# Block 2's opening shared out over three engines, fewer waits around attention, and a weight stream in five slots of eight atoms

## The reference, cut to what matters

```python
for i in range(DEPTH):                      # DEPTH = 2
    a_l = modulate(rms_norm(h_lat, norm_g[i, 0]), sh1, sc1)
    a_c = modulate(rms_norm(h_ctx, norm_g[i, 0]), csh1, csc1)
    # i == 0: y = pool_mix(a) for both sides; i == 1: attention, latents ask, both sides answer
    h_lat = h_lat + g1 * y_l
    h_lat = h_lat + g2 * sq_relu_mlp(modulate(rms_norm(h_lat, norm_g[i, 1]), sh2, sc2))
    # i == 0: the same for h_ctx
return rms_norm(h_lat, final_g)
# pool_mix: moving average over tokens minus the token, then a 256x256 product per group of columns
```

## Time and profile before

| | us |
|---|---|
| median of 3 runs | 1922.51 (1916.69 to 1923.26) |
| the profiled execution's own time | 1923.36 |
| its span, first to last instruction | 1921.5 |
| PE busy | 1795.2 (93%) |
| POOL busy | 1131.5 (59%) |
| ACT busy, DVE busy | 868.5 (45%), 834.1 (43%) |
| mean granted clock of PE | 0.963 of full |
| stream | 463 fetches of 640 KB, 3.9 us from issue to landing |

### The profile page before, as it was taken

One profiled execution on the slowest core, in us unless ns is written; L12 is line 12 of the kernel. 1 busy time (PEld: TensorE's weight loads), 2 busy tenths in 40 slices (PEclk: granted clock), 3 DMA queues, 4 the chain that ended last, 5 costly groups with the idle time before them and its releaser, 6 DMA issues.

```text
span 1921.5 us, 32487 instructions
## 1 busy us (share of the span) xinstructions
PE 1795.2 (93%) x13080; PEld 1630.0 (85%) x13080; DVE 834.1 (43%) x1970; ACT 868.5 (45%) x1364; POOL 1131.5 (59%) x611
## 2 busy tenths in 40 slices
PE   6889999999998899999999879999999889889997
PEld 5878899999998788999999757777787677679997
DVE  7677435313365775443334852121212445542223
ACT  5535546444665355464446753222323333454443
POOL 5666568778786665778887314343433323147884
PEclk9889999999998999999999979999999889989999
DMA  6453355655464534656555224433445433125552
GB/s 244 144 212 114 124 208 176 239 179 180 164 219 141 203 124 137 235 177 222 180 190 193 97 96 164 151 137 137 151 165 205 178 142 114 33 83 175 182 180 90
DMA packets 70167, 311.51 MB, mean 162 GB/s; under 512 B 7680, under 2 KB 9984, under 8 KB 69760
## 3 DMA queue, kind: packets, MB, share of 16 engines
q1 hardware_dynamic: 68400, 306.47, 46.4%
q10 hardware_dynamic: 1616, 2.95, 0.5%
HBM read 308.34 MB, written 1.05 MB: 161 GB/s over the span
## 4 chain that ended last, share of the span: by engine, by line
PE 76%; DVE 8%; POOL 4%; ACT 3%; DMA 3%; issue 3%; DVEq 2%; ACTq 0%; SPq 0%
PE bank L909 23%; PE bank L913 22%; PE bank L912 22%; POOL wlo L869 4%; DMA raw<-in_stream 3%; PE bank L924 2%; DVE split_acts L1756 1%; ACT whi L1306 1%; PE bank L932 1%; PE bank L1076 1%; PE bank L1106 1%; PE bank L1090 1%; DVE acts L2334 0%; ACT bank L1351 0%; PE bank L1238 0%
## 5 line engine op out<-in xcount | busy, mean ns | idle before, releaser
L869 POOL TENSOR_TENSOR wlo<-raw,whi 128x320 fp32r<-128x320 f32 (+1 forms) x607 | 1131.3, 1888 | 769.0 <-ACT whi L1306 768.2
L909 PE MATMUL bank<-split_acts,whi 128*128 128x256 f32 (+1 forms) x3540 | 1086.0, 307 | 53.3 <-DVE split_acts L1756 31.9
L912 PE MATMUL bank<-split_acts,whi 128*128 128x256 f32 (+1 forms) x3540 | 1068.8, 302 | 0.0
L913 PE MATMUL bank<-split_acts,wlo 128*128 128x256 f32 (+1 forms) x3540 | 1068.3, 302 | 0.0
L909 PEld LDWEIGHTS bank<-split_acts,whi 128*128 128x128 f32 x3540 | 685.2, 194 | 110.5 <-issue 48.6
L913 PEld LDWEIGHTS bank<-split_acts,wlo 128*128 128x128 f32 x3540 | 686.4, 194 | 22.0
L912 PEld LDWEIGHTS bank<-split_acts,whi 128*128 128x128 f32 x3540 | 687.0, 194 | 20.9
L1306 ACT ACTIVATE whi<-raw 128x1280 fp32r<-128x1280 f32 x367 | 464.3, 1268 | 510.8 <-PE bank L909 253.5
L2387 DVE SCALAR_TENSOR_TENSOR acts<-bank,acts 128x256 f32<-128x256 f32 x104 | 47.4, 482 | 230.8 <-PE bank L913 230.8
L2401 DVE TENSOR_SCALAR acts<-bank 128x512 f32<-128x512 f32 (+1 forms) x64 | 35.7, 558 | 212.3 <-PE bank L913 212.3
L1756 DVE TENSOR_TENSOR split_acts<-bank,split_acts 128x256 fp32r<-128x256 f32 (+1 forms) x204 | 94.4, 463 | 53.4 <-ACT split_acts L1447 24.3
(11 more groups left out here) (265 smaller groups left out, 1562.9 us busy)
## 6 DMA issues: line engine op xcount, KB each, us to landing
raw<-in_stream SPq DMA_DIRECT2D x463, 640.0 KB, 3.9
acts<-in_x SPq DMA_DIRECT2D x1, 1024.0 KB, 6.0
acts<-in_ctx ACTq DMA_DIRECT2D x1, 1024.0 KB, 7.8
acts<-in_const ACTq DMA_DIRECT2D x1, 1024.0 KB, 5.2
out<-acts SPq DMA_DIRECT2D x8, 128.0 KB, 2.1
acts<-in_const SPq DMA_DIRECT2D x1, 708.0 KB, 8.4
acts<-in_p ACTq DMA_DIRECT2D x2, 256.0 KB, 4.0
acts<-in_const ACTq DMA_DIRECT2D x1, 320.0 KB, 3.1
```

Of the source, the lines that this page charges most:

```text
L869: last = nc.gpsimd.tensor_tensor(wlo[slot][:, cols], raw[source][:, cols], whi[slot][:, cols].bitcast(F32), ALU.subtract)
L909: first = nc.tensor.matmul(out_ap, w_hi, hi_act(k), start=(k == 0), stop=False)
L912: nc.tensor.matmul(out_ap, w_hi, lo_act(k), start=False, stop=False)
L913: last = nc.tensor.matmul(out_ap, w_lo, hi_act(k), start=False, stop=(k == k_tiles - 1))
```

## The change

It has four parts.

1. The stream's chunks hold 8 atoms, in five slots (`AHEAD`, `SLOTS_AHEAD` and `FREE_SLOTS` = 4). All of it is 555 chunks instead of 463, and an "ada" chunk has no empty atoms left. The count of a layer's tiles is no longer rounded up.
2. Opening: the context's modulated tile lies in bank 7, one buffer, and x's squares in two banks. ACT also writes x times gain (`xg_ready`), POOL multiplies by the reciprocal, two tiles for each `pool_out` (`first_out`). The squares of the two norms behind the pooling have eight buffers and are summed by PE in eight matmuls. In the other norms of block 2 the eighth square goes to PE alone.
3. Attention layer: for a q tile ACT splits only what the tile needs, squares, and splits ahead after that. The split ahead of a norm's root stands two tiles later (t == 3). The first scores wait for key head 0 alone, those of unit 4 on for all keys, and V's copies are shared by DVE (0, 1) and ACT (2, 3).
4. The other lines replace the number of a tile's bank by one that counts through the layers.

```diff
-CHUNK_ATOMS = 10
-RING = 4
+CHUNK_ATOMS = 8
+RING = 5
-AHEAD = 3
-SLOTS_AHEAD = 3
+AHEAD = 4
+SLOTS_AHEAD = 4
...
-        pooled_sq = [sq2[:, 512 + i * 256:768 + i * 256] for i in range(4)]
+        pooled_sq = [sq2[:, i * 256:(i + 1) * 256] for i in range(KT)]
-        r_first = bank[7][:, 0:256]
+        r_first = var_first
-        x_squares = [bank[5], bank[6], bank[7]]
+        x_squares = [bank[5], bank[6]]
-        c_mod = [pr2[:, 512:768], pr2[:, 768:1024]]
+        c_mod = bank[7][:, 0:256]
+        last_sq = squares[:, 0:512]
...
+            def normed_latents():
+                pool.wait_ge(xg_ready, KT)
+                pool.wait_ge(first_ready, 1)
+                for k in range(KT):
+                    nc.gpsimd.tensor_tensor(side(h, k, 1), side(h, k, 1), r_first, ALU.mult).then_inc(first_out, 1)
...
             for n in range(N_SPLITS):
                 lo_parts(n, 4 if n in SHORT_PIECES else 1)
+                if n + 1 == first_splits:
+                    normed_latents()
...
+                    elif t[1:3] == (0, 1):
+                        for k in range(KT):
+                            pe.wait_ge(pooled_sq_ready, t[3] * KT + k + 1)
+                            last = nc.tensor.matmul(o, ones[:, 0:128], pooled_sq[k], start=(k == 0),
+                                                    stop=(k == KT - 1))
                     else:
                         norms += 1
-                        pe.wait_ge(sq2_used, norms * KT)
-                        src = sq2[:, cols]
-                    last = nc.tensor.matmul(o, ones[:, 0:128], src, start=True, stop=True)
+                        pe.wait_ge(sq2_used, norms * (KT - 1))
+                        nc.tensor.matmul(o, ones[:, 0:128], sq2[:, cols], start=True, stop=False)
+                        pe.wait_ge(sq2_ready, norms * KT)
+                        last = nc.tensor.matmul(o, ones[:, 0:128], last_sq[:, cols], start=False, stop=True)
...
-                if u in (0, 2):
+                if u in (0, 4):
                     pe.wait_ge(qkv_ready, 1 if u == 0 else 2)
...
+                if u == 0:
+                    pe.wait_ge(tiles_out, FIRST_TILE2 + FREE_BANKS + TILE_NO2[("v", 3)] + 1)
...
-                sc.activation(b[:, 0:256], tile(x, k), ACT.Square,
-                              scale=par2[:, PAR2["first_g"] + k:PAR2["first_g"] + k + 1]).then_inc(nhi_ready, 1)
+                g = par2[:, PAR2["first_g"] + k:PAR2["first_g"] + k + 1]
+                sc.activation(b[:, 0:256], tile(x, k), ACT.Square, scale=g).then_inc(nhi_ready, 1)
+                sc.activation(side(h, k, 1), tile(x, k), ACT.Copy, scale=g).then_inc(xg_ready, 1)
...
             for j in range(8):
-                ahead2(("q", j))
+                split_for((SECOND, ("q", j)))
                 if j >= 2:
                     act.wait_ge(qcol_done, j - 1)
                 act.wait_ge(gemm_done, FIRST_GEMM2 + TILE_NO2[("q", j)] + 1)
                 b = bank[(FIRST_TILE2 + TILE_NO2[("q", j)]) % N_BANKS]
                 sc.activation(tile(hsq, j % 2, 512)[:, 0:256], b[:, 0:256], ACT.Square).then_inc(hsq_ready, 1)
+                ahead2(("q", j))
                 modulate_split(1, 0, (0,), j)
...
+            for m in (2, 3):
+                t = ("v", m)
+                act.wait_ge(gemm_done, FIRST_GEMM2 + TILE_NO2[t] + 1)
+                sc.activation(tile(v2, m, 512), bank[(FIRST_TILE2 + TILE_NO2[t]) % N_BANKS][:, :], ACT.Copy)\
+                    .then_inc(tiles_out, 1)
...
-            v.reciprocal(r_first, var_first)
-            v.drain()
-            for t in range(KT):
-                v.scalar_tensor_tensor(out=side(h, t, 1), in0=tile(x, t),
-                                       scalar=par2[:, PAR2["first_g"] + t:PAR2["first_g"] + t + 1],
-                                       in1=r_first, op0=ALU.mult, op1=ALU.mult)
-            v.drain()
+            v.reciprocal(r_first, var_first).then_inc(first_ready, 1)
...
-            for k in range(KT):
-                sum_square(c_norm, k)
-            pool_out(1, 0)
-            pool_out(1, 1)
+
+            def latents_out(g):
+                dve.wait_ge(first_out, 2 * g + 2)
+                pool_out(1, g)
+
+            latents_out(0)
+            latents_out(1)
             norm_var2(c_norm)
             norm_root2(c_norm)
-            pool_out(1, 2)
-            for k in range(4):
-                sum_square(x_norm, k)
+            latents_out(2)
             for t in range(KT + 1):
                 modulate_step(0, 1, (0,), t)
                 if t == 1:
-                    pool_out(1, 3)
-                if t in (1, 3):
-                    sum_square(x_norm, t + 3)
-                    sum_square(x_norm, t + 4)
-                if t == 5:
+                    latents_out(3)
+                if t == 4:
                     norm_var2(x_norm)
...
+                    if j == 0:
+                        v.drain()
+                        v.memset(stat[:, 19:20], 0.0).then_inc(qkv_ready, 1)
...
-            for m in range(4):
+            for m in range(2):
                 v.tensor_copy(tile(v2, m, 512), arrived2(("v", m))[:, :]).then_inc(tiles_out, 1)
             v.drain()
-            v.memset(stat[:, 19:20], 0.0).then_inc(qkv_ready, 1)
```

More of the change, by code:

```diff
@@ L798, in build @@
         sq2_used = sem("sq2_used")
+        pooled_sq_ready = sem("pooled_sq_ready")
+        xg_ready, first_ready, first_out = sem("xg_ready"), sem("first_ready"), sem("first_out")
         sd2_ready = sem("sd2_ready")
@@ L871, in lo_parts @@
                 last.then_inc(lo_ready, 1)
+            def normed_latents():
[3 more added lines that the diff above has]
+                    nc.gpsimd.tensor_tensor(side(h, k, 1), side(h, k, 1), r_first, ALU.mult).then_inc(first_out, 1)
+            last_reach = max(REACH[(DEPTH - 1, t)] for t in TILES[:-1])
+            first_splits = max(NEEDED[(SECOND, ("py", 0, 3))],
+                               sum(c[0] == "split" for c in ORDER[:last_reach + 1]))
             for n in range(N_SPLITS):
                 lo_parts(n, 4 if n in SHORT_PIECES else 1)
+                if n + 1 == first_splits:
+                    normed_latents()
         @block.tensor
@@ L1147, in gemm2 @@
                         src = x_sums[:, 0:256] if t[1] == "first" else x_sums[:, 256:512]
+                        last = nc.tensor.matmul(o, ones[:, 0:128], src, start=True, stop=True)
+                    elif t[1:3] == (0, 1):
[3 more added lines that the diff above has]
+                                                    stop=(k == KT - 1))
                     else:
                         norms += 1
-                        pe.wait_ge(sq2_used, norms * KT)
-                        src = sq2[:, cols]
-                    last = nc.tensor.matmul(o, ones[:, 0:128], src, start=True, stop=True)
+                        pe.wait_ge(sq2_used, norms * (KT - 1))
+                        nc.tensor.matmul(o, ones[:, 0:128], sq2[:, cols], start=True, stop=False)
+                        pe.wait_ge(sq2_ready, norms * KT)
+                        last = nc.tensor.matmul(o, ones[:, 0:128], last_sq[:, cols], start=False, stop=True)
                 elif kind == "ada":
@@ L1442, in of_tile @@
                         act.wait_ge(gate_scaled, lay * (FF_T + 8) + t[1] * HALF_T + j + 1)
-                        sc.activation(tile(th, j % 2), half(bank[TILE_NO[t] % N_BANKS]), ACT.Tanh, scale=0.5)\
+                        sc.activation(tile(th, j % 2), half(bank[(lay * N_TILES + TILE_NO[t]) % N_BANKS]), ACT.Tanh, scale=0.5)\
                             .then_inc(gate_tanh, 1)
@@ L1446, in of_tile @@
                         act.wait_ge(hid_ready, lay * FF_T + (t[1] * HALF_T + j + 1))
-                        sc.activation(tile(h_hi, j), bank[TILE_NO[t] % N_BANKS][:, 0:256], ACT.Copy)\
+                        sc.activation(tile(h_hi, j), bank[(lay * N_TILES + TILE_NO[t]) % N_BANKS][:, 0:256], ACT.Copy)\
                             .then_inc(hhi_ready, 1)
@@ L1453, in of_tile @@
                         act.wait_ge(gate_scaled, lay * (FF_T + 8) + FF_T + j + 1)
-                        sc.activation(tile(gt, j % 2), half(bank[TILE_NO[t] % N_BANKS]), ACT.Tanh, scale=0.5)\
+                        sc.activation(tile(gt, j % 2), half(bank[(lay * N_TILES + TILE_NO[t]) % N_BANKS]), ACT.Tanh, scale=0.5)\
                             .then_inc(gate_tanh, 1)
@@ L1907, in take_before @@
                         dve.wait_ge(gemm_done, lay * N_TILES + TILE_NO[m] + 1)
-                        take_modulation(m, bank[TILE_NO[m] % N_BANKS], rows,
+                        take_modulation(m, bank[(lay * N_TILES + TILE_NO[m]) % N_BANKS], rows,
                                         lambda n, w: slice((lay * LAYER_ADA + n) * w, (lay * LAYER_ADA + n + 2) * w))
@@ L1958, in norm_rstd @@
                         if name == "ple" and lay == DEPTH - 1:
[L1959 removed]
```

(3 more changed lines are left out.)

80 lines of the change are left out of this document (39 added, 41 removed).

## The result

The changed kernel takes 1892.74 us (median; 1891.2 to 1895.52), the kernel before, run beside it, 1919.6: a ratio of 0.9862 (95% interval 0.9843 to 0.9882), 1.4% faster. The profiled execution took 1892.0 us (span 1890.2) against 1923.4 (1921.5), 31.3 us less; forecast were 24.1 less, 1899.3.

A forecast was written before the change was run, and what follows sets the result against it. PE bounds the long products; between them its idle time and the half clock that follows could be won. Terms -6.9 - 1.0 - 6.5 - 9.7 + 0 = -24.1 took 1923.4 to 1899.3 us, range 1888 to 1911.

The forecast's parts named there:

- its own sign: Wrong if the heads move by more than 8 us either way, or k0 starts less than 5 us sooner against the opening's end.
- The stream: Weight stream: dearer POOL pieces (+4.4 us) set against faster landings and one more slot; 0 in all, between -8 and +8.
- rival 3: Heads of both layers: an extra slot spares a third of the clock loss, 8 us, giving 1891.3; chance 0.14.
- Opening: Block 2's opening: context tile in bank 7, POOL normalising, fewer sums on DVE; -6.9 us, bounds -11 and 0.
- Copies at 0: Opening's loop: eight more ACT copies cost between 0 and 3.7 us; taken as 0, because ACT also waits there now.
- The rule of the Trainium skill: Opening: keep two-input elementwise work on VectorE; by it POOL's eight tiles would cost 3.2 us more if all on the path.
- Norms: Three norms in block 2: eighth square goes to PE instead of DVE's sum; -1.0 us, 0 to -2.
- Q tiles: Q tiles before k0: square ahead of the split, less waiting and half clock; -6.5 us, bounds 0 and -10.
- Rival 2: Q tiles: chunks land late all the same, so 6.5 us is lost, 1905.8; chance 0.12.
- V and attention: V and attention loop: earlier V, full clock, copies shared with ACT; -9.7 us, bounds -4 and -12.
- Rival 1: Opening and before k0: clock stays down after remaining idle stretches, 7.1 us not won, 1906.4; chance 0.17.

The follow-up runs named there:

- a_nostall: Changed kernel, with a split held back in the last pg and pp tiles when its slot is a weight chunk's; 1887.1 us, ratio 0.9836.
- b_stream: Kernel before with the stream alone changed to five slots of eight atoms (pieces of 256 columns follow); 1906.39 us, ratio 0.9936.
- a_ring4: Changed kernel with four slots of eight atoms, splits planned three ahead; 1895.61 us, ratio 0.987.
- b_pieces5: Kernel before with five pieces of 256 columns a chunk in the heads instead of four, four slots kept; 1921.06 us, ratio 1.0008.
- n_pieces2: a_nostall with two pieces of 512 columns in the heads instead of four of 256; 1898.0 us, ratio 0.988 against the kernel before.
- n_pieces8: a_nostall with eight pieces of 128 columns in the heads instead of four of 256; 1898.06 us, ratio 0.9892 against the kernel before.
- a_oldstream: Changed kernel with the old stream set back (four slots of ten atoms, four pieces of 320 columns); 1904.68 us, ratio 0.992.
- n_modsbuf: a_nostall with the modulated context tile in SBUF again instead of bank 7; 1890.03 us, ratio 0.984 against the kernel before.
- n_dvenorm: a_nostall with DVE, not POOL, multiplying the eight latent tiles by the reciprocal; 1889.85 us, ratio 0.9835 against the kernel before.

## Why the prediction was right in sum and wrong in parts

By its own sign the prediction was wrong in its division: it called itself wrong if the heads moved by more than 8 us, and the start of the pg tiles came 14.9 us sooner. The sum came out within its range because the opening's 6.9 us did not come, in place of which the new ring made a stall. Without that stall (a_nostall, 1887.1) the time is just below the range of 1888 to 1911.

**The stream (0 forecast, -14.9 measured, the start's -2.4 in it)** is the step that failed: "I set this against the 4.4: 0 in all". POOL's price was near: in its busy stretch a piece of 256 took 0.796 us (52 pieces from 24.1 to 65.5 us), 0.398 an atom for 0.385, where I had 0.414. What I had not weighed is what the late transfers cost PE. Before, ACT's time line around 61 us, and PE's below it:

```profile
61.45 0.47 ACT L1481 ACTIVATE split_acts<-bank,acts 128x256 fp32r<-128x256 f32 x1
68.84 1.27 ACT L1306 ACTIVATE whi<-raw 128x1280 fp32r<-128x1280 f32 x1 [6.92 <-DMA raw<-in_stream]
70.02 0.37 ACT L1480 ACTIVATE bank<-bank 128x256 f32<-128x256 f32 x1
```

```profile
71.67 2.07 PE L987 MATMUL bank<-acts 128*128 128x256 f32 x4 [3.46 <-DVE acts L1936]
```

ACT stands at a split; the cast of the next compressed tile waits behind it, DVE's sum waits for that, PE for DVE: 3.5 us idle, and then the clock is at 1.2 GHz (PE's busy time, granted clock, DMA share, GB/s of that stretch, before):

```profile
70.70:84.40 13.70, 11.25 (x40) 0.50 0.55 205
```

After, in the same place:

```profile
65.04 1.06 ACT L1328 ACTIVATE whi<-raw 128x1024 fp32r<-128x1024 f32 x1 [7.08 <-DMA raw<-in_stream]
```

```profile
67.66 1.07 PE L937 MATMUL bank<-raw,acts 128*32 128x256 f32 x16 [0.73 <-DVE acts L1963]
69.26 1.13 PE L1000 MATMUL bank<-acts 128*128 128x256 f32 x4 [0.54 <-DVE acts L1964]
```

ACT waits as long, but it ends 3.8 us sooner, and PE's two waits sum to 1.3. Over head 0 PE's idle time fell from 18.9 to 17.0 us, and its busy time, with the same 1604 matmuls, from 207.4 to 203.2. So 4.2 of the head's 6.1 us are faster matmuls, that is clock. The granted clock agrees in its direction (30.7 us at half clock before, 13.7 after) but is no measure of the size: b_stream's head 0 is as short with 20.5. This is rival 3, given 0.14 and 8 us; that its 1891.3 lies next to the measured time is luck, since the gain was larger and the stall took the difference. It needs both the fifth slot (a_ring4, b_pieces5: 225 to 227) and pieces of 256 (n_pieces2 227, n_pieces8 224); the eight kernels with both lie at 219.3 to 221.0. The wait at this place divides them in the same way: 3.0 to 3.8 us in the four kernels with four slots, 2.3 and 2.1 with pieces of 512 and of 128, and two short waits of 1.6 or less together in the eight. For layer 1's stretch the eight spread over 518.1 to 522.0, so up to 4 us there are chance. Why slot and piece are needed together is not shown beyond this.

**Start (-2.4, a part of the -14.9, not forecast).** DVE's chain of tiny operations ahead of the first matmul waits for POOL. Time line of DVE before, then POOL's:

```profile
7.09 0.17 DVE L1777 TENSOR_SCALAR acts<-acts 128x8 f32<-128x8 f32 x1
7.34 2.46 DVE L1780 SCALAR_TENSOR_TENSOR acts<-acts 128x8 f32<-128x8 f32 x3
...
11.18 0.81 DVE L1787 SCALAR_TENSOR_TENSOR acts<-acts 128x8 f32<-128x8 f32 x1
```

```profile
7.29 3.31 POOL L869 TENSOR_TENSOR wlo<-raw,whi 128x320 fp32r<-128x320 f32 x4 [6.85 <-ACT whi L1306]
11.10 3.31 POOL L869 TENSOR_TENSOR wlo<-raw,whi 128x320 fp32r<-128x320 f32 x4 [0.51 <-ACT whi L1306]
```

An operation of 0.17 us lasts 0.81 here: it began 0.08 us behind the start of a POOL piece and ended 0.02 us behind that piece's end. POOL's pieces follow each other every 0.82 us. After, L1815, L1857 and L1859 ran in the pause between POOL's two chunks, at 0.17 each. How the two chains meet differs from run to run: with pieces of 256 and five slots the first matmul came at 12.7 to 14.4 us in eight kernels, with pieces of 320 at 15.1 and 15.1, so the gain is 0.7 to 2.4 us.

**Opening (-6.9, measured +0.3).** Up to the reciprocal (L2459, now L2487) it took 45.0 us and takes 49.6; I had -2.4. The stall is 5.9 of it (a_nostall: 43.7, a_oldstream 43.6). The rest, -1.3 without the stall, is my step less a clock that I could not see: from the last pp matmul to L2298 it was 6.2 us and is 3.7 in a_nostall, -2.5 as forecast, but PE ran the loop's first 3.4 us at half clock. The bank alone is worth about 1.7, by one profile each (n_modsbuf 45.4, a_nostall 43.7). "Copies at 0" held: from the first pg matmul to the last pp matmul it takes 24.06 us in after and 24.05 in b_pieces5, which has no copies, both with 3.4 us at half clock. From the reciprocal to w1 it took 32.9 and takes 28.7: -4.2 for the -4.5 forecast (29.6 in a_nostall, where the held-back split stands in this stretch). The first pooled outputs behind POOL, after:

```profile
1087.60 5.58 POOL L879 TENSOR_TENSOR acts<-acts 128x256 f32<-128x256 f32 x8 [18.41 <-DVE acts L2487]
```

```profile
1089.13 0.88 DVE L2459 SCALAR_TENSOR_TENSOR acts<-bank,acts 128x256 f32<-128x256 f32 x2 [1.68 <-POOL acts L879]
```

DVE goes on 1.7 us behind the reciprocal's end, for the 1.6 forecast. The rule of the Trainium skill (GPSIMD Engine Reference, Engine selection) that was weighed there: POOL's eight took 5.58 us for DVE's 3.22, 1.7 times as long where the page says about twice, and yet keeping them on DVE costs 0.7 us (n_dvenorm), since only two of them stand on the path.

**Norms (-1.0, measured 0).** The column "to q" holds the one with 512 columns: 396.9 both times. I let the first added matmul run beside the sum; it does not. PE waits for the sum of seven, which ended 0.12 us behind the last square, and has both matmuls behind it, 0.94 us more where I had 0.47:

```profile
1503.86 1.10 PE L1170 MATMUL bank<-acts 128*128 128x512 f32 x2 [0.29 <-issue]
1504.80 1.02 PE L1172 MATMUL bank<-acts 128*128 128x512 f32 x2
```

In the others, with 256 columns, PE's wait fell from 1.7 to 1.2 us and the matmul of 0.47 took that back.

**Q tiles (-6.5, measured -8.7).** Right in kind; a_oldstream and b_stream show that order and stream remove the same wait. Rival 2 (the chunks land late all the same) is out: ACT's waits there fell from 8.00 and 5.64 to 1.8 and 1.0:

```profile
1541.28 1.07 ACT L1328 ACTIVATE whi<-raw 128x1024 fp32r<-128x1024 f32 x1 [1.84 <-DMA raw<-in_stream]
...
1549.30 1.06 ACT L1328 ACTIVATE whi<-raw 128x1024 fp32r<-128x1024 f32 x1 [0.98 <-DMA raw<-in_stream]
```

**V and attention (-9.7, measured -8.3).** V's start: 36.5 us behind k0 before, 34.2 after, -2.3 for -3.7; the missing 1.4 is half clock, which covered the first 2.2 us from k0 on before and the first 5.1 after. V itself took 25.05 and takes 23.27, -1.8 (-1.6 forecast). The first maximum behind V (unit 2; those of units 0 and 1 come ahead of V's end in both kernels) came 4.9 us behind V's end and comes 1.5 behind it, -3.4 as forecast:

```profile
1614.80 1.29 DVE L2593 COPY acts<-bank 128x512 f32<-128x512 f32 x2 [6.26 <-PE bank L1259]
...
1616.25 0.69 DVE L2550 CUSTOM_DVE_ANT_0 acts<-bank,acts 128x512 f32<-128x512 f32 x1
```

Where the k tiles had full clock (a_nostall) the stage gave -10.7. Rival 1 thus took about 1.4 us here and 1.4 in the opening, not 7.1.

## What to carry to other kernels

When a ring changes its number of slots, look up anew which earlier chunk each prefetch has to wait for: an engine that stands in order at such a chunk holds everything behind it. Price a late transfer by what stands behind the waiting engine, and add the half clock that follows PE's gap. Where one engine's short operation has to wait for the end of another's running piece, the length of a piece has two prices: long pieces stall the one engine, short ones load the other. Here four pieces of 256 columns did better than two or eight by 11 us each; other lengths were not run.

## What the runs showed of the hardware

While POOL works, a two-operand DVE operation with all operands in SBUF waits for the end of POOL's running piece and then does its own work. It ends behind that piece by 0.02 us with 8 columns, 0.28 with 256, 0.55 with 512 and 1.08 with 1024 (medians, the same in before and after). A tiny operation of 0.17 us thus becomes 0.74 to 0.83 beside pieces of 320 columns. One-input TENSOR_SCALAR operations wait too (0.15 us behind the end with 256 columns), RECIPROCALs do not: 19 of 128x1 that began beside a running piece in before took 0.15 to 0.17 us. A low part of 256 columns took a mean of 1004 ns from SBUF and 420 with an operand in a bank. Alone, POOL's two-input operation took 0.69 us for 256 columns, 0.83 for 320 and 2.40 for 1024: some 0.13 us and 2.2 ns a column, where I had read 0.25 and 2.11 out of rows beside DVE.
